# Router logits of the last two token tiles taken from the transposed residual itself, in a fused two-layer generator kernel

## The reference, cut to what matters

```
xl = xl + mod_l[:, 2] * yl                       # after the output projection
h2l = modulate(rms_norm(xl, norm_g[i, 1]), mod_l[:, 3], mod_l[:, 4])
    # rms_norm(x, g) = x * rsqrt(mean(x * x) + 1e-6) * g ;  modulate(h, b, s) = h * (1 + s) + b
scores = sigmoid(h @ router_w)                   # 32 per token, in 8 groups of 4
biased = scores + router_b                       # best group, two best experts in it
y = sum over the chosen experts of combine * (silu(h @ w_gate[e]) * (h @ w_up[e])) @ w_down[e]
xl = xl + mod_l[:, 5] * y
```

## Time and profile before

| what | value |
|---|---|
| median of 3 runs | 990.14 us (988.76 to 990.9) |
| the profiled execution | 988.34 us, its span 986.5 us |
| TensorE busy | 859.6 us, 87% of the span |
| VectorE, ScalarE, GpSimd busy | 323.5, 164.2, 174.5 us |
| mean granted clock of TensorE | 0.949 of full |
| DMA | 297.99 MB, 302 GB/s over the span |

### The profile page before, as it was taken

One profiled execution on the slowest core, in us unless ns is written; L12 is line 12 of the kernel. 1 busy time (PEld: TensorE's weight loads), 2 busy tenths in 40 slices (PEclk: granted clock), 3 DMA queues, 4 the chain that ended last, 5 costly groups with the idle time before them and its releaser, 6 DMA issues.

```text
span 986.5 us, 10011 instructions
## 1 busy us (share of the span) xinstructions
PE 859.6 (87%) x3779; PEld 378.4 (38%) x3779; DVE 323.5 (33%) x707; ACT 164.2 (17%) x401; POOL 174.5 (18%) x212
## 2 busy tenths in 40 slices
PE   1899989996899999868769999898796999978786
PEld 0444435444533333222247444354545333322222
DVE  1269995314321222110232432647205111111110
ACT  2301022213100000000032112445303000000000
POOL 2100391131211222211212211201111111110101
PEclk9899998998999999989979999999896899988898
DMA  9989453627898999999989033454737799999993
GB/s 365 405 358 395 155 221 138 256 86 242 314 407 336 357 399 395 394 402 420 407 350 387 0 125 131 184 243 170 298 130 256 298 399 414 412 421 425 414 422 153
DMA packets 33110, 297.99 MB, mean 302 GB/s; under 512 B 6464, under 2 KB 6770, under 8 KB 16156
## 3 DMA queue, kind: packets, MB, share of 16 engines
q1 hardware_dynamic: 26064, 283.26, 71.3%
q0 software_dynamic: 6912, 13.92, 4.1%
q10 hardware_dynamic: 76, 0.02, 0.0%
HBM read 293.66 MB, written 12.58 MB: 310 GB/s over the span
## 4 chain that ended last, share of the span: by engine, by line
PE 63%; DMA 15%; issue 6%; DVE 5%; ACT 3%; POOL 3%; SPq 2%; PEld 1%; another core or an unknown queue 0%; PEldq 0%; DVEq 0%; POOLq 0%; ACTq 0%
PE bank L1129 16%; PE bank L468 9%; DMA ring<-in_gu_pack 8%; PE bank L1152 7%; PE bank L1222 6%; PE bank L1272 5%; DMA B<-in_gu_pack 4%; PE bank L958 3%; PE bank L1033 3%; PE bank L1235 2%; SPq L907 2%; DMA ring<-in_mod_pack 2%; PE bank L997 2%; PE bank L1080 1%; POOL GB L2100 1%
## 5 line engine op out<-in xcount | busy, mean ns | idle before, releaser
L1129 PE MATMUL bank<-ring,hT 128*64 128x512 f32 x688 | 207.9, 626 | 21.8 <-issue 12.3
L1877 DVE SCALAR_TENSOR_TENSOR hT<-hT,WORK,bank 128x256 f32<-128x256 f32 x34 | 16.3, 480 | 325.6 <-ACT hT L1405 312.8
L1129 PEld LDWEIGHTS bank<-ring,hT 128*64 128x64 f32 x688 | 61.7, 143 | 115.8 <-issue 115.5
L1963 DVE SCALAR_TENSOR_TENSOR WORK<-WORK,par 128x512 f32<-128x512 f32 x116 | 90.7, 860 | 0.0
L468 PE MATMUL bank<-ring,hT 128*128 128x512 f32 (+2 forms) x256 | 88.0, 499 | 0.7 <-ACT hT L1378 0.7
L1152 PE MATMUL bank<-ring,WORK 128*64 128x512 f32 x368 | 83.5, 595 | 1.6 <-ACT WORK L1410 1.6
L1129 PE MATMUL bank<-WORK,hT 128*64 128x512 f32 x128 | 63.1, 638 | 8.9 <-issue 7.3
L958 PE MATMUL bank<-ring,cs 128*32 128x512 f32 x384 | 49.0, 643 | 15.5 <-DMA ring<-in_mod_pack 8.2
L1222 PE MATMUL bank<-hT,ring 128*128 128x512 f32 x128 | 58.9, 620 | 1.8 <-ACT hT L1459 1.8
L468 PEld LDWEIGHTS bank<-ring,hT 128*128 128x128 f32 x256 | 46.0, 190 | 35.8 <-issue 34.0
L1410 ACT ACTIVATE WORK<-bank 128x256 f32<-128x256 f32 x34 | 13.1, 384 | 280.2 <-PE bank L1138 269.2
(11 more groups left out here) (273 smaller groups left out, 1045.6 us busy)
## 6 DMA issues: line engine op xcount, KB each, us to landing
ring<-in_gu_pack SPq DMA_DIRECT2D x42, 2048.0 KB, 17.4
ring<-in_mod_pack SPq DMA_DIRECT2D x24, 2048.0 KB, 16.6
ring<-in_down_pack SPq DMA_DIRECT2D x22, 2048.0 KB, 26.0
WORK<-in_gu_pack SPq DMA_DIRECT2D x6, 2048.0 KB, 30.5
ring<-in_wout_pack SPq DMA_DIRECT2D x4, 2048.0 KB, 14.1
ring<-in_win_pack SPq DMA_DIRECT2D x3, 2048.0 KB, 37.8
X<-in_gu_pack SPq DMA_DIRECT2D x3, 2048.0 KB
B<-in_gu_pack SPq DMA_DIRECT2D x3, 2048.0 KB
```

Source lines behind the costliest of these rows:

```text
L1129: mm = pe.matmul(dst[ST * x:ST * x + ST, :], HG[L][s][:, k, :], columns(units[x], 512 * k, 512), start=k == 0, stop=k == KC - 1)
L1963: ins = dve.scalar_tensor_tensor(out=acc, in0=src, scalar=w, in1=acc, op0=ALU.mult, op1=ALU.add)
```

## The change

The logits of the last two tiles (in layer 1: of both) come from transposes of the unscaled residual, multiplied with router weights that hold the channel factor; the row factor and the shift's share are put in afterwards, on 32 numbers a token. The normed tiles are made beside the router, for the experts only. With this go:

- `turn_raw` on PE: 16 transposes of `X` into the banks 4 to 7, read by three ACT copies and one DVE copy (`raw_cols`, `raw_logits`) into `B[:, 2048:4096]`.
- `raw_weights` on DVE, ahead of the projection's end: one 128x256 multiply.
- the shift's share: 8 matmuls with the shift as stationary operand, one DVE copy of 32 columns.
- In layer 0 the first two tiles keep the old way, and half of their transposes move in front of the projection's last four matmuls; ACT and DVE still share their eight pieces.
- The eight pieces of the last two tiles are all read by ACT, after the sigmoid; the copies of the rows follow on ACT, in layer 0 two of them between the first and the second four pieces.
- The last residual add moves from POOL to DVE.
- The stores of the last two tiles' rows wait for all rows; the first gather's halves wait each for its half.
- SP's `X` place also waits for the transposes and the raw logits, since it overwrites their sources.
- The second buffer of the gated product moves to `MR`; some semaphores are joined.

The diff, cut to its core:

```diff
+            def turn_raw(L, j):
+                pe.wait_ge(sem("x_added"), (7, 11)[L] + j)
+                for h in range(2):
+                    for k in range(4):
+                        mm = pe.transpose(bank[RAW_BANKS[j][h]][:, k * P:(k + 1) * P], X[:, 2 + j, 512 * h + k * P:512 * h + (k + 1) * P], ident)
+                    mm.then_inc(sem("raw_turned"), 1)
...
             def route(L):
...
+                if L == 0:
+                    for i in range(2):
+                        pe.wait_ge(sem(f"ht_{i}"), ht_before("m0", i) + 4)
+                    logits(0, rw, lambda k: hT[:, k, 0:HALF], 1)
+                pe.wait_ge(sem("raw_cols_0"), 3 * L + 1)
                 for k in range(KC):
+                    pe.matmul(bank[4][:, 0:EXPERTS], mods[:, L, 3, k, 1:2].to_broadcast([P, P]), rw[:, k, :], start=k == 0, stop=k == KC - 1)
+                pe.wait_ge(sem("raw_cols_0"), 3 * L + 3)
+                pe.wait_ge(sem("raw_cols_1"), L + 1)
+                logits(1, rws, lambda k: B[:, 2048:4096].rearrange("p (j k t) -> p k j t", j=2, k=KC)[:, k], 2 * L + 2)
+                if L == 0:
+                    turn_logits(1, 2, (0, 1))
+                turn_logits((2, 3)[L], 3, (nt - 2, nt - 1))
...
+                turn_last(f"m{L}", range(4))
+                if L == 0:
+                    h_rows(range(2))
+                turn_last(f"m{L}", range(4, KC))
+                h_rows(range(2, 4) if L == 0 else range(2))
...
                     mm.then_inc(sem("ranks"), 1)
-                h_rows(range(nt // 2, nt))
+                h_rows(range(2 * nt - 4 + 2 * L, 2 * nt))
...
                 for h in range(2):
+                    pe.wait_ge(sem("h2_rows"), 8 * L + 2 * nt - 2 + 2 * h)
...
+                    if i == 7 and k == 6:
+                        turn_pair("m0", 0, range(4))
                     mm = out_half(i, (k,))
                 mm.then_inc(sem("out_mm"), 1)
-            turn_x("m0", range(4))
+            turn_pair("m0", 0, range(4, KC))
+            turn_raw(0, 0)
+            turn_raw(0, 1)
```

```diff
+            def raw_logits(L):        # on DVE
+                nt = moe_plan(L)[0]
+                dve.wait_ge(sem("raw_turned"), 4 * L + 4)
+                dve.tensor_copy(RAWT[1][:, 512:1024], bank[RAW_BANKS[1][1]][:, :]).then_inc(sem("raw_cols_1"), 1)
+                scaled(f"m{L}", nt - 2)
+                dve.wait_ge(sem("logit_parts"), L + 2)
+                link(dve.tensor_copy(shifted, bank[4][:, 0:EXPERTS]))
+                scaled(f"m{L}", nt - 1)
+                dve.wait_ge(sem("logits"), L + 2)
+                score = routing(L)["score"]
+                for j in range(2):
+                    ins = dve.scalar_tensor_tensor(out=score[:, 32 * (nt - 2 + j):32 * (nt - 1 + j)], in0=bank[3][:, 32 * j:32 * j + 32],
+                                                   scalar=rstd[:, 2 + j:3 + j], in1=shifted, op0=ALU.mult, op1=ALU.add)
+                ins.then_inc(sem("raw_scaled"), 1)
...
                 for t in range(nt):           # on POOL, experts(L)
-                    pool.wait_ge(sem("h2_rows"), 8 * L + 2 * t + 2)
+                    pool.wait_ge(sem("h2_rows"), 8 * L + (2 * t + 2 if t < nt - 2 else 2 * nt))
...
                     sp.wait_ge(sem("xs"), (8, 14)[L])          # on SP, the X place
+                    sp.wait_ge(sem("raw_turned"), 4 * L + 4)
+                    sp.wait_ge(sem("logit_parts"), L + 2)
```

More of the change, by code:

```diff
@@ L674, in attention_scalar, with moe_scalar, h_rows @@
             mod_copy(11)
-        def moe_scalar(act, L, gate_rows, experts):
+        def moe_scalar(act, L, gate_rows, hcols, experts):
             nt, c, over, ntile = moe_plan(L)
[L679 to L685, removed]
+            score = routing(L)["score"]
+            if L == 0:
+                act.wait_ge(sem("logit_parts"), 1)
+                act.activation(MR[:, 0, 0:HALF], bank[0][:, 0:HALF], ACT.Copy).then_inc(sem("logit_rows"), 1)
+            act.wait_ge(sem("logit_parts"), L + 2)
+            act.activation(MR[:, 0, nt * P - HALF:nt * P], bank[1][:, 0:HALF], ACT.Copy).then_inc(sem("logit_rows"), 1)
+            if L == 0:
+                act.wait_ge(sem("logits"), 1)
+                act.activation(score[:, 0:64], bank[2][:, 0:64], ACT.Sigmoid)
+            act.wait_ge(sem("raw_scaled"), L + 1)
+            act.activation(score[:, 32 * (nt - 2):32 * nt], score[:, 32 * (nt - 2):32 * nt], ACT.Sigmoid).then_inc(sem("scored"), 1)
+            H2 = h2_order(nt)
+            def h_rows(part):
+                for n in part:
+                    t, h = H2[n]
+                    act.wait_ge(sem("h2_turned"), 8 * L + n + 1)
+                    act.activation(B[:, 1024 * t + 512 * h:1024 * t + 512 * h + 512], bank[2 * (n % 2)][:, :], ACT.Copy).then_inc(sem("h2_rows"), 1)
+            hcols(f"m{L}", 1 - L, range(4), LAST_BANKS)
+            if L == 0:
+                h_rows(range(2))
+            hcols(f"m{L}", 1 - L, range(4, KC), LAST_BANKS)
+            h_rows(range(2 - 2 * L, 2 * nt))
             for h in range(2):
@@ L696, in moe_scalar, with h2_order @@
             overflow_scalar(act, L)
+        def h2_order(nt):
+            return [(t, h) for t in range(nt - 2) for h in (0, 1)] + [(t, h) for h in (0, 1) for t in (nt - 2, nt - 1)]
         def second_tile(eng, L, g):
@@ L1046, in route @@
[L1046 to L1059, removed]
@@ L1061, in route, with logits, turn_logits @@
-                h_rows(range(nt // 2))
+                def logits(b, weights, src, n):
+                    for k in range(KC):
+                        mm = pe.matmul(bank[b][32 * (k % 4):32 * (k % 4) + 32, 0:HALF], weights[:, k, :], src(k), start=k < 4, stop=k >= 4)
+                    mm.then_inc(sem("logit_parts"), 1)
+                def turn_logits(n, b, tiles):
+                    pe.wait_ge(sem("logit_rows"), n)
+                    for j, t in enumerate(tiles):
+                        mm = pe.matmul(bank[b][:, j * 32:j * 32 + 32], MR[:, 0, t * P:(t + 1) * P], C("sel32"), start=True, stop=True)
+                    mm.then_inc(sem("logits"), 1)
@@ L1206, in _ @@
             mod(0)
-            turn_x("a0", range(4))
+            turn_x("a0")
             mod(1)
```

202 lines of the change are left out of this document (130 added, 72 removed).

## The result

The changed kernel takes 977.69 us (median of 4 runs, 975.18 to 980.88), the kernel before on the same chip 989.45 (988.44 to 990.9): a ratio of 0.9867, 95% interval 0.983 to 0.9904. The forecast was 977.1. The profiled execution took 980.07 us, its span 978.4. So the sum came out; its two terms did not, as the stages show, so the good total is luck. I count each layer from the first row of the last gated product (L1743 before, L1867 after), which starts when the projection has ended: 224.69 and 739.84 before, 225.17 and 735.89 after. I call these points zero; +24.8 means 24.8 us behind zero. In layer 0 the new zero itself stands behind the 8 transposes that moved in front of the last projection matmuls (1.04 us), so that what is gained from zero on is 1.04 more than what is gained in all.

What follows compares the result with a forecast made beforehand. TensorE and DMA were both taken as nearly full, with TensorE's shift deciding layer 0 and the weight stream's restart layer 1. Gains 4.4 + 8.6 = 13.0 off 988.34 gave 975.3; less 1.8 profile offset, 977.1 us; range 973.5 to 983.5.

Steps and rivals of the forecast that it cites:

- 4.4 earlier: Layer 0: the first gather starts at 243.3 instead of 247.67 us, and this shift passes through whole to the end.
- The rival of a falling clock in layer 0: TensorE's clock falls before layer 0's gather: 9.2 us lost; with layer 1 cold too, 990.6 us; chance 0.05.
- the rival of a clock that falls there: Layer 1's clock still falls before the gather, leaving only 4.35 us there: 981.4 us in all; chance 0.25.
- with 7.5, 762.2: Layer 1: the second row store, issued at 754.7, lands in 7.5 us, so the next lent place starts at 762.2.
- 8.6 earlier: Layer 1: the weight stream runs continuous from 767.2 instead of 775.84 us, and the kernel's end moves with it.
- The store's price: Layer 1's 512 KB stores: 6.4 to 8.6 us to landing from the trace, against 3.2 estimated from the skill.
- The sum of 14.6: Both layers' gain if the skill's 3.2 us store price held, with layer 1 then giving 10.2 us.
- The longer chain from ACT: Rival, both layers: PE and ACT waits or slow raw-path hand-overs lose 1 to 2 us a layer; 980 us; chance 0.12.
- The cold gather in layer 0: The rival of a falling clock in layer 0: its gather takes 14.1 instead of 7.38 us; chance 0.05.
- The uncarried shift in layer 0: Rival: layer 0's stream is full already, so only the `B` place's 2 us pass; 979.5 us; chance 0.05.

Runs made afterwards that it cites:

- again: The changed kernel once more, nothing edited; 976.47 us, ratio 0.9847 to the kernel before.
- old_again: The kernel before the change, unchanged, measured and profiled a second time; 991.69 us, ratio 1.0007.
- old_warm: The kernel before, with 53 idle transposes added in layer 1 where TensorE waits anyway; 986.21 us, ratio 0.9956.
- l0_only: The changed kernel with layer 1 put back to its old order, layer 0 as changed; 979.41 us, ratio 0.9887 to the kernel before.
- early_parts: The changed kernel, with three pieces of a lent place started right behind the `X` place in both layers; 975.08 us, ratio 0.9851 to the kernel before.
- early_parts2: The same kernel as early_parts, measured again beside the unedited changed kernel; 974.24 us, ratio 0.9821 to the kernel before.
- x_late: The changed kernel, with SP's `X` place in layer 1 waiting until the rows are stored; 974.79 us, ratio 0.9836 to the kernel before.
- l0_delay: The changed kernel with 26 idle transposes right ahead of layer 0's first gather; 980.63 us, ratio 0.9879 to the kernel before.

## Why the prediction was right in its sum and wrong in its terms

**Layer 0, to the gather.** The forecast was a sigmoid at +9.4 behind the shifted end of the projection and a gather at +17.8. The rows have +8.4 and +16.5 (+15.85 in the other profiles without a delay), where the kernel before has +23.0. So the gather is 6.5 to 7.1 earlier from zero on, and 5.4 to 6.1 in all. The single durations were right: shift matmuls 1.97 (2.2 forecast), ACT from the sigmoid's end to its last row copy 9.0 (9.1). What I over-priced were the hand-overs: I set each step behind the other on TensorE, 1 us too long in sum. From the sigmoid to the gather I had 8.35; it is 8.2 here, behind transposes slowed by the clock, and 7.5 in again.

**Layer 0, the clock.** The forecast took layer 0's old gather as 7.38 us at 2.4 GHz from the one profile at hand. The old order does not hold that clock in each execution. The timeline and two stretches of old_again:

```profile
247.98 9.71 PE L1080 MATMUL bank<-WORK,B 128*128 128x128 f32 x64 [0.73 <-issue]
```

```profile
246.00:248.00 2.00, 1.27 (x7) 0.50 0.91 371
...
254.00:256.00 2.00, 2.00 (x21) 1.00 0.00 0
```

The clock fell before the gather, which took 9.71 (9.24 in old_warm, whose layer 0 is the old one), and the layer was 278.1 and 273.5 us long where the first profile has 271.7. In the new order it fell before the gather in one profile of eleven, the one shown at the top (8.22 instead of 7.31). So the failed step is the term "**4.4 earlier**" of layer 0: measured 11.2 us (8.5 to 13.9) by l0_only, of which 5.4 to 6.1 is the earlier gather, and the rest goes with the falls of the clock that the old order has more often. In old_again and old_warm the gather began only at +24.7 and +24.9, and SP started the `B` place at +34.5 and +34.3, where the first profile has +30.5 and the new order about +28.5. The DMA engines then stood still, as in this stretch of old_again at +30 (0.71 in the first profile):

```profile
253.28:258.28 5.00, 5.00 (x44) 4.56 (x44) 0.00 (x0) 1.15 (x2) 0.00 (x0) 1.00 0.00 0
```

How much each fall costs was not measured by itself. The rival of a falling clock in layer 0 asks what busy share keeps it ("about 6 of 10 us"); no run shows such a bound, and the pair of 3.14 and 3.16 of 5 us above speaks against a busy share that decides by itself.

**Layer 1, to the ring.** The gather's clock and its 3.68 us (3.7 forecast) were right, its start better (5.5 earlier, 4.35 forecast), and with them the rival of a clock that falls there is out: 1.00 in each stretch up to +30. TensorE freed the places 11.3 earlier (10.2 forecast), but SP started them only 9.4 earlier, for the lent place stood ahead of them in its list.

**Layer 1, the stream.** The failed step is "with 7.5, 762.2" and what hangs on it, "the stream is continuous from 767.2 where it was from 775.84: **8.6 earlier**". Two parts of it failed. The landing took 10.7 and not 7.5, because the stores now come right behind the `X` place's 2 MB; so the lent place started where it had been, and 2.4 of the 8.6 were gone. And the hole that was left in the old stream, from the place's end at about +30 to 775.84 (+36), was not empty: the stretches from +30 to +40 had shares of 0.44 and 0.71, so that filling them gave 4.25. The restart of the stream was the wrong measure, idle DMA time the better one. Over all 14 profiles layer 1's length less its idle time from +10 to +40 is 235.9 to 237.9, while the idle time itself goes from 3.6 and 3.9 (early_parts, early_parts2) over 5.3 to 6.8 (the new order and old_warm) to 10.7 (the three with the old layer 1).

**The store's price.** With the `X` place kept behind them layer 1's stores took 3.5 us in the median (x_late), with its 2 MB ahead 10.2, the last one 10.7. The estimate of 3.2 us from the Trainium skill, *DMA: Bandwidth & Descriptors*, section "Anatomy of one DMA — SWDGE (gpsimd) path", is nearer to the first than I gave it credit for, and says nothing of the second. The sum of 14.6 that I worked out from it is not borne out: x_late, with the short landing and a later `X` place, is no clear gain over the changed kernel.

**The other rivals.** The longer chain from ACT: the reverse was seen. The cold gather in layer 0: it came once, as a part (0.9 us), not for 9.2. The uncarried shift in layer 0 (2 us pass): refuted by the 11.2 of l0_only, whose interval begins at 8.5; l0_delay agrees.

So the right total came from two errors that happened to cancel: layer 1 gave 4.5 less than forecast and layer 0 some 4 to 7 more. What stays open is what decides, between two executions of the same instructions, whether the clock falls.

## What to carry to other kernels

In a stage that streams the same bytes in each version, don't ask when the stream restarts, but how much DMA time is idle between two fixed points, and take the share stretch by stretch. An edit gains what it fills, but only where no later wait gives it back: early_parts filled idle time in both layers, shortened layer 1 by 1.0 to 3.3 us and layer 0 not at all. In layer 1 a lent buffer filled in pieces was worth about as much as a TensorE that starts 5.7 us sooner, which is worth 0.7 to 2.2. Look also at the order of the list of transfers: a place that is free gains nothing while one that is not stands ahead of it. And one profile does not tell which clock an order holds: look at two or three before the clock enters a sum.

## What the runs showed of the hardware

A small store that is issued behind a large transfer waits for it: two stores of 512 KB took 10.2 us in the median to land when 2 MB were issued just ahead of them, 3.5 when those came after. TensorE's clock differs between executions of the same instructions with the same busy time ahead (3.14 and 3.16 of 5 us: 1.00 and 0.66 behind it), and once low it can stay so under work without a stop: in old_again this stretch was at 1.2 GHz throughout.

```profile
250.00:252.00 2.00, 2.00 (x12) 0.50 0.67 274
```

The Trainium skill, *TensorE: Matmul & The Clock Gate*, section "What's actually happening", says that activity releases the throttle; it did, by 254.
